# Streaming the first modulation by feature groups, with the first two column chunks in step, in a two-block sequence kernel

## What is computed

```
cond = silu(c)
mod = cond @ w_ada + b_ada                       # 6 x 2048 values
sh1, sc1, g1, sh2, sc2, g2 = split(mod, 6)
h = x * (1 + sc1) + sh1                          # 256 x 2048
z = h @ w_in + b_in                              # 2048 x 9216 weights
z_u, z_v, z_h, z_g = split(z)
filt = hyena_filters(...)                        # depends on no input x
k = [h_fwd with h_bwd[0] added, 0, reversed h_bwd]; spectrum of k
```

## Time and profile before

| | |
|---|---|
| median of three runs | 2793.67 us |
| the profiled execution | 2792.58 us |
| its span (first to last instruction) | 2791.3 us |
| TensorE matmul busy | 2671.2 us, 96% |
| VectorE busy | 1794.2 us, 64% |
| ScalarE busy | 1268.7 us, 45% |
| GpSimd busy | 67.5 us, 2% |
| DMA, mean over the span | 215 GB/s |

### The profile page before, as it was taken

How to read it: one execution, slowest core, us unless ns; L and a number is a source line. 1 busy time by engine, 2 the same in 40 slices (tenths; PEclk the granted TensorE clock), 3 DMA queues, 4 the chain that set the end, 5 groups by cost and what they waited for, 6 DMA issues and landing times.

```text
span 2791.3 us, 31507 instructions
## 1 busy us (share of the span) xinstructions
PE 2671.2 (96%) x12605; PEld 2210.3 (79%) x12605; DVE 1794.2 (64%) x1797; ACT 1268.7 (45%) x1538; POOL 67.5 (2%) x67
## 2 busy tenths in 40 slices
PE   2679999999999999999999999999999999999999
PEld 1368997777877888888888788888888888888887
DVE  6666866776888664458677755555554565656665
ACT  0044443333434444465555443444444465556464
POOL 2300000000000000000000000000000000000000
PEclk9789999999999999999999999999999999999999
DMA  8688667777977775556565555555565555543554
GB/s 316 245 304 299 236 213 249 267 256 267 347 268 252 272 260 190 181 192 205 194 196 196 185 188 170 166 181 181 183 219 194 195 181 180 175 133 124 200 185 143
DMA packets 258084, 599.45 MB, mean 215 GB/s; under 512 B 12244, under 2 KB 14943, under 8 KB 243423
## 3 DMA queue, kind: packets, MB, share of 16 engines
q1 hardware_dynamic: 246848, 561.55, 59.3%
q0 software_dynamic: 4848, 23.64, 2.5%
q10 hardware_dynamic: 6254, 12.40, 1.3%
HBM read 587.07 MB, written 10.49 MB: 214 GB/s over the span
## 4 chain that ended last, share of the span: by engine, by line
PE 89%; DVE 7%; ACT 1%; issue 1%; DMA 1%; POOL 1%; ACTq 0%; DVEq 0%; POOLq 0%
PE ps L787 26%; PE ps L789 25%; PE ps L788 25%; DVE ada_acc L2003 2%; PE ps L887 2%; PE ps L871 1%; PE ps L874 1%; PE ps L873 1%; DVE w_lo L1975 1%; PE ps L1032 1%; PE ps L1023 1%; PE ps L948 1%; PE ps L904 1%; DMA raw<-in_w_in 0%; DMA rows_d<-in_ln_b 0%
## 5 line engine op out<-in xcount | busy, mean ns | idle before, releaser
L1975 DVE TENSOR_TENSOR w_lo<-raw,w_hi 128x1024 fp32r<-128x1024 f32 x870 | 1051.8, 1222 | 767.4 <-ACT w_hi L1376 766.0
L1376 ACT CAST w_hi<-raw 128x1024 fp32r<-128x1024 f32 x870 | 907.5, 1051 | 1119.1 <-PE ps L789 1008.3
L787 PE MATMUL ps<-w_lo,x_hi 128*128 128x512 f32 x2592 | 1020.6, 394 | 8.8 <-DVE w_lo L1975 4.9
L789 PE MATMUL ps<-w_hi,x_lo 128*128 128x512 f32 x2592 | 1011.6, 390 | 0.0
L788 PE MATMUL ps<-w_hi,x_hi 128*128 128x512 f32 x2592 | 1011.2, 390 | 0.0
L787 PEld LDWEIGHTS ps<-w_lo,x_hi 128*128 128x128 f32 x2592 | 488.4, 188 | 112.3 <-issue 8.0
L789 PEld LDWEIGHTS ps<-w_hi,x_lo 128*128 128x128 f32 x2592 | 488.1, 188 | 102.7
L788 PEld LDWEIGHTS ps<-w_hi,x_hi 128*128 128x128 f32 x2592 | 488.3, 188 | 100.6 <-issue 1.2
L2003 DVE SCALAR_TENSOR_TENSOR ada_acc<-raw,cond,ada_acc 128x2048 f32<-128x2048 f32 x96 | 236.1, 2460 | 3.5 <-DVE ada_acc L2003 0.5
L787 PE MATMUL ps<-w_lo,pooled_hi 128*128 128x512 f32 x384 | 151.0, 393 | 2.5 <-DVE w_lo L1975 2.5
L789 PE MATMUL ps<-w_hi,pooled_lo 128*128 128x512 f32 x384 | 149.5, 389 | 0.0
(11 more groups left out here) (340 smaller groups left out, 2064.0 us busy)
## 6 DMA issues: line engine op xcount, KB each, us to landing
raw<-in_w_m SPq DMA_DIRECT2D x128, 1024.0 KB, 5.3
raw<-in_w_ada SPq DMA_DIRECT2D x96, 1024.0 KB, 5.0
raw<-in_w_in SPq DMA_DIRECT2D x72, 1024.0 KB, 5.7
raw<-in_pool_w_in SPq DMA_DIRECT2D x64, 1024.0 KB, 5.4
raw<-in_pool_w_out SPq DMA_DIRECT2D x32, 1024.0 KB, 5.0
raw<-in_ple_w_gate SPq DMA_DIRECT2D x32, 1024.0 KB, 5.1
raw<-in_mla_w_in SPq DMA_DIRECT2D x24, 1024.0 KB, 5.1
raw<-in_w_o SPq DMA_DIRECT2D x16, 1024.0 KB, 6.5
```

Of the source, the lines that this page charges most:

```text
L787: mm(bank, xh, wl, start=start, stop=False)
L789: ins = mm(bank, xl, wh, start=False, stop=stop)
L1376: nc.scalar.copy(by_ktile(st, w_hi[st.half_slot(j, half)][:, 0:n]), raw_half(st, j, half)).then_inc(hi_split, 1)
L1975: tt(by_ktile(st, w_lo[slot][:, 0:n]), raw_half(st, j, half), by_ktile(st, w_hi[slot][:, 0:n].bitcast(F32)), ALU.subtract).then_inc(lo_spl ...
```

## The change

The first two modulation blocks are no longer summed whole before anything else. Stage "ada" is gone; stage "first" takes the 2048 features of shift and scale in four groups of 512. Each group has eight "a" units, each made of two loads of 512 KB (one k-tile, both blocks, 512 columns), and two "w" units: the group's four k-tiles of column chunks 0 and 1 of `w_in`. So chunks 0 and 1 are accumulated in PSUM over the four groups, and "in_vu" is left with chunks 2 and 3. Four "a" units of the later blocks go from "in_vu" to "in_h2".

x is turned at the start, before it is scaled, and kept in `xT`; VectorE now scales and shifts it (`group_scale`) and forms `x_lo` in halves (`group_lo`), and ScalarE rounds in halves. The filters' sum and difference are formed in PSUM: the hidden layer times forward weights plus (minus, with a negated hidden layer) the hidden layer times backward weights. GpSimd's two operations go; the steps at `w3` double from 4 to 8 matmuls for each filter, and each product, each window step and each of the two transforms is handed on by itself. The condition vector is loaded first by a load of its own, `b_ada` comes as rows and is added by VectorE, the rope tables move to the pooling stage, and the window, transform and gating matrices are loaded by GpSimd's queue.

```diff
-    ("ada", 8, [("aaaa", "")]),
-    ("in_vu", 2, [("ww", "awwa")] * 2), ("in_h", 2, A2), ("in_h2", 1, W2), ("in_g", 4, A2),
+    ("first", 1, [("aaaaaawwaa", "")] * 4),
+    ("in_vu", 1, [("ww", "awwa")] * 2), ("in_h", 2, A2), ("in_h2", 1, A2), ("in_g", 4, A2),
...
+                q, k = u // 8, 2 * (u % 8)
+                load(st, 0, j, tuple(w_mod[:, k + e, 0:2, cols(q)] for e in range(2)))
...
-            then(nc.gpsimd.tensor_tensor(h_sum[:], h_fwd[:], h_bwd[:], ALU.add))
-            nc.gpsimd.tensor_tensor(h_bwd[:], h_fwd[:], h_bwd[:], ALU.subtract).then_inc(filt_sum, 1)
...
+        def filter_product(it, d):
             o, c = it // 2, it % 2
+            if it + d:
+                pe.wait_ge(filt_win, 2 * it + d)
+            for t in range(2):
+                fwd, bwd = (w3[0:HID, (2 * e + o) * W1 + c * CH:(2 * e + o) * W1 + (c + 1) * CH] for e in range(2))
+                part = slice(t * P, (t + 1) * P)
+                mm(ps[:, 4 + t, :], hid_arg[0:HID, part], fwd, start=True, stop=False)
+                ins = mm(ps[:, 4 + t, :], (hid_n if d else hid_arg)[0:HID, part], bwd, start=False, stop=True)
+            ins.then_inc(filt_mm, 1)
+
+        def spectrum(it, m):
+            pe.wait_ge(filt_win, 2 * it + m + 1)
+            if it + m:
+                pe.wait_ge(spec_copied, 2 * it + m)
...
+        def group_sum(q):
+            pe.wait_ge(filt_win, 2 * q + 2)
+            pe.wait_ge(ada_added, 8 * (q + 1))
+            for n in range(8):
+                ins = mm(ps[:, 4, n:n + 1], group_acc[q % 2][:, n * P:(n + 1) * P], ones[:, 0:1], start=True, stop=True)
+            ins.then_inc(group_summed, 1)
+
+        st = ST["first"]
+        for q in range(4):
+            if q == 1:
...
+            filter_product(q, 0)
+            filter_product(q, 1)
+            spectrum(q, 0)
+            spectrum(q, 1)
+            group_sum(q)
+            for c in range(2):
                 for half in range(2):
...
+                    pe.wait_ge(fm_lo if half else h_lo, q + 1)
+                    products(st, 0, 10 * q + 6 + c, half, 4 * q + 2 * half, x_hi, x_lo, pair(c),
+                             q == 0 and half == 0, q == 3 and half == 1)
...
+        act.wait_ge(c_turned, 1)
+        nc.scalar.activation(sig_c[:], ps[:, 4, 0:KT], ACT.Sigmoid).then_inc(c_sig, 1)
+        act.dma_start(w3[0:HID, :], a["hy_w3"][0]).then_inc(hidden_in, 16)
+        act.dma_start(freq[:], a["k_freq"][0].partition_broadcast(P)).then_inc(hidden_in, 16)
         for dst, src in vectors:
             act.dma_start(dst, src).then_inc(vectors_in, 16)
...
+        EARLY = {1: vectors_turned, 2: lambda: hidden(0), 3: lambda: hidden(1), 4: negate_hidden}
+        for q in range(4):
+            for u in range(6):
+                add_first(q, u)
+                if q == 0:
+                    EARLY.get(u, lambda: None)()
+                elif u == 0:
+                    group_scale(q - 1)
+                elif u == 1:
+                    group_lo(q - 1)
+            filter_part(q, 0)
+            for c in range(2):
+                rest_unit(ST["first"], 0, 10 * q + 6 + c)
+            filter_part(q, 1)
+            for u in (6, 7):
+                add_first(q, u)
+        group_scale(3)
+        group_lo(3)
```

More of the change, by code:

```diff
@@ L92 @@
 ]
+FIRST_LOADS = 40
 class Stage:
@@ L128, in landed, with parts @@
     def landed(self, i, j):
-        return self._line(lambda r: 16 * ((self.first + r * self.length + j) // SLOTS + 1), i)
+        def parts(n):
+            return sum(2 if m < FIRST_LOADS and self.kinds[m] == "a" else 1 for m in range(n % SLOTS, n + 1, SLOTS))
+        return self._line(lambda r: 16 * parts(self.first + r * self.length + j), i)
     def freed(self, kind, i, j):
@@ L194, in block_kernel @@
     acc = [at("ada_acc0", 112, [D]), at("ada_acc1", 120, [D])]
+    group_acc = [at(f"group_acc{i}", 112 + 4 * i, [2 * CH]) for i in range(2)]
     dft = at("dft", 128, [4, 2, S])
@@ new lines, in add_first @@
+        def add_first(q, u):
+            st, j = ST["first"], 10 * q + (u if u < 6 else u + 2)
+            dve.wait_ge(raw_full[st.slot(j)], st.landed(0, j))
+            if u:
+                dve.wait_ge(ada_added, 8 * q + u)
+            elif q >= 2:
+                dve.wait_ge(group_summed, q - 1)
+            buf = group_acc[q % 2]
+            for e in range(2):
+                part = raw[st.slot(j)][:, e * 2 * CH:(e + 1) * 2 * CH]
+                gain = cond[:, 2 * u + e:2 * u + e + 1]
+                if u + e == 0:
+                    ins = tsc(buf[:], part, gain, None, ALU.mult)
+                else:
+                    ins = stt(out=buf[:], in0=part, scalar=gain, in1=buf[:], op0=ALU.mult, op1=ALU.add)
+                if e == 0:
+                    then(ins)
+            ins.then_inc(ada_added, 1)
```

382 lines of the change are left out of this document (202 added, 180 removed).

## The result

The changed kernel takes 2799.42 us (median of 20 runs, 2793.75 to 2803.87), the kernel before 2794.44 (median of 20 runs, 2792.71 to 2796.61): ratio 1.0018, 95% interval 1.0011 to 1.0025. That is 5.0 us slower than before, just within the 0.2% that count as no change here (the interval reaches over it), where 4.8 us faster were forecast: 10.5 us above 2788.9, and inside the range. The profiled executions of the experiments lie up to 4.4 us to either side of their medians, so lengths read from one trace carry that much doubt.

What follows compares the result with a forecast made beforehand. TensorE, busy 96% of the span, was taken as the bound. Chunks 0 and 1 complete at 75.2 + 122.7 + 13.2 = 211.1, 4.8 us earlier than before, gave a median of 2788.9 us, range 2774 to 2801.

Steps and rivals of the forecast that it cites:

- chunks 0 and 1 complete at 215.9 before: Kernel before, ahead of "in_h": two column chunks take 43.5 us before 259.4, so both are complete at 215.9.
- the three groups: From the first products to the last group's: three groups of 40.9 us each, 122.7 together.
- I take 23, bounds 20 and 27.: Start: the last small vector lands at 23 us, with `w3` now ahead of 17 of them; before, 20.9.
- The way from the vectors to the first product, 52.2: Start: vector steps to 20 us, then 32.2 at half clock; first product at 23 + 52.2 = 75.2.
- One group at full clock, 34.6: From one group's first product to the next's: TensorE's steps, waits and hand-offs sum to 34.6 us.
- The clock, 6.3 in a group: Each group: second product half 1.7, first transform 2.3, restart behind sums 2.3; loss 6.3 us, bounds 2.3 and 10.9.
- the clock is lost: Rival, in groups: both transforms wholly at 0.50, 4.6 us more in each of three, 2802.7 us; chance 0.13.
- The clock holds: Rival, in groups: only the restart behind the sums is lost, 36.9 us a group, 2776.9 us in all; chance 0.22.
- VectorE and the loads are faster: In a group: VectorE needs 31 us, loads 29, both under 40.9; without TensorE's line a group would cost 31.
- Last products: After the three groups: the last products take 10.9 + 2.3 = 13.2 us, completing chunks 0 and 1 at 211.1.
- the rest of the program at 0: Later stages: four units moved to "in_h2" cost 0, at most 2 us; rope tables in pooling cost 0.
- The late vectors: Rival, at the start: vectors land at 30 us instead of 23, giving 2795.9 us; chance 0.10.

Runs made afterwards that it cites:

- g0_start: Changed kernel with vectors first on ScalarE's queue, `w3` in eight pieces behind, x loaded at once, window, transform and gate matrices held behind the vectors: 2786.18 us.
- a2_fill: Changed kernel with five unread 512-column products put into TensorE's pause between a group's sums and its products: 2788.78 us, ratio 0.9978.
- c1_pool_late: Changed kernel with GpSimd's queue issuing its loads, x included, only when the vectors have landed; `w3` stays ahead of them: 2794.11 us, ratio 1.0001.
- a3_quarter: Changed kernel with TensorE's filter work cut in groups 2 to 4, the first group's filter product halved, hand-offs kept, output incomplete: 2773.39 us.
- f1_stack: Changed kernel with the filter product over all 128 rows of TensorE, one matmul in place of two of 64 rows: 2767.99 us, ratio 0.9905.
- g1_all: Changed kernel with altered load order at the start, 128-row filter products, sums between the transforms and ScalarE's rounded x before the second spectrum's copy: 2760.92 us.

## Why the prediction was wrong, point by point

- **Measuring from the first matmul of "in_h", and chunks 0 and 1 complete at 215.9 before.** Right. The forecast for it was 254.6, the profiled execution has 267.9. The 13.3 between them are all accounted for: the vectors 10.5, the way from there to the first product -0.7, the three groups 3.5 (126.2 against 122.7).
- **"I take 23, bounds 20 and 27."** This is the step that failed. It was 33.5, outside its own bounds and outside the rival's 30. The forecast asked what stood ahead of the vectors in ScalarE's queue, `w3`, and priced that at 2 us; it named the transforms and the window in the rival's list but did not ask what had kept them from the vectors before: they had been on ScalarE's queue behind the vectors, and the change issues them on another queue at 5 us. Nor did it count that the vectors are themselves issued later, the last one at 12.7 us instead of 9.6. With the loads' order mended (`g0_start`) the kernel is within 2.7 us of the forecast, and with that kernel's 17.4 put in for 23 the sum gives 2783.3, 2.9 under what was measured. 2788.9 + 10.5 is 2799.4, the measured median; the landing is known only for the profiled execution, though, and the 15.3 that it missed its own 2787.8 by are the 13.3 above and 2 of the tail.
- **The way from the vectors to the first product, 52.2.** Right, 51.5; with vectors at 17.4 it was 54.7, since a unit's load, not the vectors, then ended VectorE's wait, until 30.5.
- **One group at full clock, 34.6.** Right: 34.2 in the only group that ran at full clock throughout (`a2_fill`).
- **The clock, 6.3 in a group.** Right in kind and place (the second filter product at half clock, the clock back inside the first transform, the products' start at half clock), and a little too small in size. The second product lost 2.3 to 3.5 us (taken as 1.7), the transform 1.3 to 2.7 (2.3), the restart about 2 (2.3). In all, with 2.6 and -2.6 set aside the groups' mean is 42.1 in the profiled execution against 40.9, and 40.6 in `g0_start`. Against the 34.2 at full clock the loss is 7.9 and 6.4, so the profiled execution stands at the very point (7.9) from which the rival "the clock is lost" was to decide, without what it named: the second transform stayed at full clock in every group. "The clock holds" occurred in two groups, from 116.6 to 153.0 in `g0_start` and from 124.9 to 161.3 in `c1_pool_late`: 36.4 us each, where the forecast had 36.9 for that case. Why these two held is open.
- **VectorE and the loads are faster, cover without TensorE's line 31.** Right in order, but no kernel came down to 31: `a3_quarter`, `f1_stack` and `g1_all` have groups of 33 to 35 (37 in the first, with the gating matrix), in which VectorE still waits for TensorE's first filter product or its sums while TensorE waits for VectorE's last unit. The two orders hand over to each other at both ends.
- **Last products, the rest of the program at 0.** Right within the 2 us of the tail.
- **The chances.** The late vectors, at 0.10 and with 7 us, were the case that happened; with the measured 10.5 for its 7 its sum is the measured time. The rival of the lost clock, 2802.7, was 3.3 off on the other side, and its mechanism did not occur. The sum of the chances for slower is 0.14 (0.13 and a tenth of 0.10), not 0.15, and that for the same 0.41. Of the signs of being wrong, one came, a first group of 43.9 us against 43, but the forecast's own sum had 43.5 for that group, so it told nothing.

## What to carry to other kernels

A small transfer is late not only by what is ahead of it in its own queue: when a load is moved to another queue and so into the same microseconds, count one of its packets ahead of every small one, and look for what kept it away before. A pause of TensorE costs its length and the restart at half clock; fill it with real work, and turn the order of every engine that hands over there, not TensorE's alone. Here it paid to stack products that use half of TensorE's rows, twice over since their clock no longer fell.

## What the runs showed of the hardware that I had not expected

- TensorE's clock fell while it was at work and stayed low while it was busy without a pause: from 107 to 117 us of the changed kernel it was busy 10.00 of 10.00 us with 64-row filter products and the transform behind them, at a granted 0.52; from 97 to 107, at 0.97, it had been busy 7.58 of 10.00. The same product over 128 rows (`f1_stack`) stayed at 1.00 from 89 to 100 us, with TensorE busy 8.58 of 11.00 us. The 64-row products don't always lose it: single groups of `a2_fill`, `c1_pool_late` and `g0_start` kept full clock through them.
- Five products in each group that nobody reads made the kernel 10.6 us faster.
- The DMA engines' share of busy time stayed at 0.99 to 1.08 while what they moved went from 375 to 213 and back to 349 GB/s. The share alone does not show that loads are slow.
- Runs of the changed kernel lie 10 us apart (2793.75 to 2803.87, 20 runs), those of the kernel before 4 (20 runs), and those of `f1_stack` 1.4 (only four runs). In the changed kernel the time goes with the mean granted clock of the run, 0.982 at 2793.75 and 0.978 at 2803.87; why a run gets more or less of it was not tried.
